# The causal mask of an attention layer cut to its two diagonal squares

## What is computed

```python
def causal_block_attention(q, k, v):
    nb = S_ // Q_BLOCK                       # 256 // 128
    def one_block(args):
        qi, bi = args
        s = jnp.einsum('bqhd,bkhd->bhqk', qi, k).astype(jnp.float32) * scale
        qpos = bi * Q_BLOCK + jnp.arange(Q_BLOCK)
        s = jnp.where(kpos[None, :] <= qpos[:, None], s, -jnp.inf)
        p = jax.nn.softmax(s, axis=-1).astype(v.dtype)
        return jnp.einsum('bhqk,bkhd->bqhd', p, v)
```

## Time and profile before

| | us |
|---|---|
| median of 3 runs | 2367.28 |
| lowest and highest | 2366.36, 2370.49 |
| the profiled execution | 2367.2 |
| its span, first to last instruction | 2365.5 |
| TensorE busy | 2327.2 |
| VectorE busy | 1439.8 |
| ScalarE busy | 1064.5 |

### The profile page before, as it was taken

How to read it: one execution, slowest core, us unless ns; L and a number is a source line. 1 busy time by engine, 2 the same in 40 slices (tenths; PEclk the granted TensorE clock), 3 DMA queues, 4 the chain that set the end, 5 groups by cost and what they waited for, 6 DMA issues and landing times.

```text
span 2365.5 us, 37140 instructions
## 1 busy us (share of the span) xinstructions
PE 2327.2 (98%) x14529; PEld 2024.2 (86%) x14535; DVE 1439.8 (61%) x1559; ACT 1064.5 (45%) x1372; POOL 223.3 (9%) x231
## 2 busy tenths in 40 slices
PE   8999989999999999999999999998999999999999
PEld 7898878888888888888989899887888888888887
DVE  6664567556546556567667767565755555555556
ACT  4455454434434434445544536344443443443442
POOL 0052001001001001000012211110100000000000
PEclk9999999999999999999999999999999999999999
DMA  6664456665665665655533435254666656656654
GB/s 235 195 170 123 148 192 199 200 192 184 196 189 183 198 195 179 199 201 169 171 117 117 145 89 170 85 183 152 196 191 193 189 192 190 191 190 231 187 193 137
DMA packets 236683, 417.25 MB, mean 176 GB/s; under 512 B 23761, under 2 KB 46570, under 8 KB 234986
## 3 DMA queue, kind: packets, MB, share of 16 engines
q1 hardware_dynamic: 235162, 410.73, 55.5%
q10 hardware_dynamic: 1360, 4.19, 0.5%
HBM read 412.77 MB, written 2.10 MB: 175 GB/s over the span
## 4 chain that ended last, share of the span: by engine, by line
PE 90%; DVE 5%; ACT 2%; issue 1%; POOL 1%; DMA 0%; ACTq 0%; POOLq 0%; DVEq 0%
PE quad L642 20%; PE quad L667 13%; PE quad L668 13%; PE quad L669 13%; PE quad L645 10%; PE quad L613 4%; PE quad L615 4%; PE quad L617 4%; DVE wlo L1685 1%; DVE cv L2146 1%; ACT whi L1263 1%; PE quad L1136 1%; PE quad L720 1%; PE quad L810 1%; PE quad L884 1%
## 5 line engine op out<-in xcount | busy, mean ns | idle before, releaser
L1685 DVE TENSOR_TENSOR wlo<-raw,whi 128x1024 fp32r<-128x1024 f32 x760 | 979.2, 1296 | 688.6 <-ACT whi L1263 686.5
L1263 ACT ACTIVATE whi<-raw 128x1024 fp32r<-128x1024 f32 x760 | 800.5, 1058 | 972.9 <-PE quad L669 495.8
L642 PE MATMUL quad<-xs,whi 128*128 128x512 f32 x2048 | 649.3, 397 | 7.1 <-DVE xs L2006 6.2
L667 PE MATMUL quad<-whi,hh 128*128 128x512 f32 x1248 | 488.7, 392 | 1.0 <-POOL hl L2363 1.0
L669 PE MATMUL quad<-whi,hl 128*128 128x512 f32 x1248 | 485.8, 389 | 0.0
L668 PE MATMUL quad<-wlo,hh 128*128 128x512 f32 x1248 | 485.7, 389 | 0.0
L645 PEld LDWEIGHTS quad<-xs,wlo 128*128 128x128 f32 x2048 | 386.8, 189 | 91.4 <-issue 0.3
L645 PE MATMUL quad<-xs,wlo 128*128 128x256 f32 x2048 | 404.0, 279 | 0.6 <-issue 0.6
L642 PEld LDWEIGHTS quad<-xs,whi 128*128 128x128 f32 x2048 | 314.4, 190 | 9.1 <-issue 7.3
L667 PEld LDWEIGHTS quad<-whi,hh 128*128 128x128 f32 x1248 | 234.3, 188 | 49.7 <-POOL hl L2363 1.4
L669 PEld LDWEIGHTS quad<-whi,hl 128*128 128x128 f32 x1248 | 234.3, 188 | 49.3
(11 more groups left out here) (320 smaller groups left out, 2123.5 us busy)
## 6 DMA issues: line engine op xcount, KB each, us to landing
raw<-in_mlp_w SPq DMA_DIRECT2D x512, 512.0 KB
raw<-in_gdn_w_in SPq DMA_DIRECT2D x105, 512.0 KB
raw<-in_w_out SPq DMA_DIRECT2D x64, 512.0 KB
raw<-in_mem_w_kv SPq DMA_DIRECT2D x32, 512.0 KB
raw<-in_mla_w_in SPq DMA_DIRECT2D x25, 512.0 KB
raw<-in_mla_w_ukv SPq DMA_DIRECT2D x24, 256.0 KB
gb<-in_ln_g SPq DMA_DIRECT2D x4, 1024.0 KB, 7.0
gb<-in_ln_b SPq DMA_DIRECT2D x4, 1024.0 KB, 9.1
```

Of the source, the lines that this page charges most:

```text
L642: last = nc.tensor.matmul(both, b.whi[:, slot, k, cols], b.xs[:, :, kt, :], start=start, stop=stop, skip_group_check=True)
L667: nc.tensor.matmul(ps[:, t, 0:n], ah[:, kt, toks], hi[:, k, 0:n], start=start, stop=False)
L1263: nc.scalar.activation(b.whi[:, c % NSPLIT], b.raw[:, slot], ACT.Copy).then_inc(sem.hi_ready, 1)
L1685: nc.vector.tensor_tensor(b.wlo[:, c % NSPLIT], b.raw[:, c % NRAW], b.whi[:, c % NSPLIT].bitcast(F32), ALU.subtract).then_inc(sem.lo_ready, 1)
```

## The change

The mask `causal` shrinks from 128 x 2 x 256 to one square of 128 x 128, the same for both tiles, as each tile's diagonal square is the same. In `scores` the mask is added by two matmuls per head, each over the 128 columns of a tile's diagonal square, the second one between the scores of tile 0 and tile 1. The square of tile 0 by keys 128 to 255 is no longer written. A new function `keys` gives how many keys a tile has, and maximum, exponential and division of tile 0 take 128 instead of 256 columns in causal heads; the maximum becomes one reduction per tile there.

```diff
+def keys(n, t):
+
+    return (t + 1) * P if NM <= n < NM + NH else S
...
-    b.causal, o = at("causal", [P, TT, S], BF16, o)
+    b.causal, o = at("causal", [P, P], BF16, o)
...
-                if causal:
-                    nc.tensor.matmul(ps[:, :], b.identb[:, :], b.causal[:, :, :].rearrange("p t s -> p (t s)"),
-                                     start=True, stop=False, skip_group_check=True)
                 for t in range(TT):
                     toks = slice(t * P, (t + 1) * P)
                     nk = P * (t + 1) if causal else S
+                    if causal:
+                        nc.tensor.matmul(ps[:, t * S + nk - P:t * S + nk], b.identb[:, :], b.causal[:, :], start=t == 0,
+                                         stop=False, skip_group_check=True)
...
                 for t in range(TT):
-                    last = nc.scalar.activation(b.prob[:, n % 2, t, :], turn_ps[n % 2][:, t * S:(t + 1) * S], ACT.Exp,
+                    k = keys(n, t)
+                    last = nc.scalar.activation(b.prob[:, n % 2, t, 0:k], turn_ps[n % 2][:, t * S:t * S + k], ACT.Exp,
...
-                nc.vector.tensor_reduce(b.mx[:, n % 2, :], turn_ps[n % 2][:, :].rearrange("p (t s) -> p t s", t=TT), AX.X,
-                                        ALU.max, negate=True).then_inc(sem.bias_set, 1)
+                if keys(n, 0) == S:
+                    nc.vector.tensor_reduce(b.mx[:, n % 2, :], turn_ps[n % 2][:, :].rearrange("p (t s) -> p t s", t=TT), AX.X,
+                                            ALU.max, negate=True).then_inc(sem.bias_set, 1)
+                    return
+                for t in range(TT):
+                    last = nc.vector.tensor_reduce(b.mx[:, n % 2, t:t + 1], turn_ps[n % 2][:, t * S:t * S + keys(n, t)], AX.X,
+                                                   ALU.max, negate=True)
+                last.then_inc(sem.bias_set, 1)
...
                 for t in range(TT):
-                    last = nc.vector.tensor_scalar(b.prob[:, n % 2, t, :], b.prob[:, n % 2, t, :],
+                    k = keys(n, t)
+                    last = nc.vector.tensor_scalar(b.prob[:, n % 2, t, 0:k], b.prob[:, n % 2, t, 0:k],
                                                    b.rinv[:, n % 2, t:t + 1], None, ALU.mult)
...
-            link(nc.gpsimd.memset(b.causal[:, :, :], 0.0))
+            link(nc.gpsimd.memset(b.causal[:, :], 0.0))
```

More of the change, by code:

```diff
@@ L2351, in _ @@
                     nc.gpsimd.engine_nop().then_inc(sem.const_set, 1)
-            link(nc.gpsimd.memset(b.causal[:, :, :], 0.0))
-            link(nc.gpsimd.affine_select(out=b.causal[:, :, :], in_=b.causal[:, :, :], compare_op=ALU.is_ge, fill=NEG,
-                                         base=0, pattern=[[P, TT], [-1, S]], channel_multiplier=1))
+            link(nc.gpsimd.memset(b.causal[:, :], 0.0))
+            link(nc.gpsimd.affine_select(out=b.causal[:, :], in_=b.causal[:, :], compare_op=ALU.is_ge, fill=NEG,
+                                         base=0, pattern=[[-1, P]], channel_multiplier=1))
             freq = 1.0 / (np.float32(ROPE_THETA) ** (np.arange(0, ROPE, 2, dtype=np.float32) / np.float32(ROPE)))
```

## The result

The changed kernel takes 2372.39 us (median of 22 executions, 2369.60 to 2377.34), the kernel before, timed beside it, 2368.18 (22, 2366.14 to 2370.49). The ratio is 1.0021, 95% interval 1.0014 to 1.0028: slower by 4.2 us (3.3 to 6.6 by the interval), just over the 0.2% that I had called the limit of "no change", and above my range, which ended at 2370.0. Its profiled execution took 2370.82 us, with a span of 2369.1, 3.6 more than before.

What follows compares the result with a forecast made beforehand. TensorE's queue was taken as the bound (busy 98% of the span); masks at -0.06 to +0.06 us and all other parts at nothing summed to 0.0 us, so 2367.2 us, range 2365.0 to 2370.0.

Steps and rivals of the forecast that it cites:

- the limit of "no change": Whole kernel: about 0.2% (4.7 us) is what a measurement can tell from no change; chance of staying within, 0.92.
- The bound of the stage: Twelve causal heads: bound by TensorE's steps, busy 75.34 of 76.00 us, with only a 0.2 us weight-load wait.
- The price of the masks: Causal heads, TensorE: 24 small masks at 0.104 to 0.109 us replace twelve at 0.213; net -0.06 to +0.06 us.
- Rival (a): Causal heads: each small mask costs only its own columns, 0.053 us, giving 2365.9 us; chance 0.25.
- Rival (b): Causal heads: the bf16-to-fp32 weight switch is not hidden, 0.34 us per mask, +5.7 us, giving 2372.9; chance 0.03.
- Maximum, exponential, division: Causal heads, VectorE and ScalarE: changed work lies beside TensorE's path and turns into waiting; counted as no time.
- Rival (d): Freed ScalarE and VectorE time reaches the end after all, at most 5.0 us, giving 2362.2; chance in full 0.01.
- One causal step still 5.24 us long: Expected sign in the changed profile: the distance from one causal head's step to the next stays 5.24 us.
- the 0.1 us of the forecast: Causal-head stage: main forecast of no difference beyond 0.1 us; chance 0.58.
- nothing in the trace depends on an address: Buffers behind `causal` move down 768 bytes a partition; no row prices this, so it was taken as zero.
- The signs of failure: Total off over 3 us with unchanged steps: clock or outside-stage reasoning wrong; step shorter by over 0.1 us: weight-load bound wrong.
- The clock, rival (c): Half-clock stretches after layer norms may shift over other work, -2.1 to +1.3 us each; chance of visible shift 0.11.

Runs made afterwards that it cites:

- vec_only: Changed kernel with TensorE's old 512-column mask and old mask buffer, keeping the new maximum, exponential and division; 2368.57 us, ratio 1.0004 to the kernel before.
- b_pad24: Kernel before with 48 satisfied waits (24 instructions) added ahead of TensorE's first matmul; 2372.30 us, ratio 1.0018.
- a_pad16: Changed kernel with 32 satisfied waits (16 instructions) added ahead of TensorE's first matmul; 2372.13 us, ratio 1.0017 to the kernel before.
- a_pad32: Changed kernel with 64 satisfied waits (32 instructions) added ahead of TensorE's first matmul; 2367.50 us, ratio 0.9995 to the kernel before.

## Why the prediction was wrong

- **The bound of the stage** was right: TensorE at 75.45 of 76 us, no new wait.
- **The price of the masks** was right: 0.11 us each, the scores of a head 0.005 us longer, where I had -0.005 to +0.005. Rival (a), its own columns only, is false where fp32 weights follow, and true where bf16 weights do. Rival (b), a switch that isn't hidden, is false: 0.11 and not 0.34 us. Its total of 2372.9 is near the measured 2372.39 by luck, for a reason that isn't there.
- **Maximum, exponential, division** at nothing was right: `vec_only` 1.0004 [0.9995, 1.0013], and the saved time stands in ScalarE's wait, 2.76 against 2.61 us. Rival (d) is false.
- **"One causal step still 5.24 us long"** was wrong by a little: it became 5.28. The excess is not in the masks but in the 12 matmuls of the output chunk behind them, which take 230 ns from start to start instead of 227. It makes 0.26 us from the first head's mask to the last one's (68.20 against 67.94), more than the 0.1 us of the forecast.
- **The step that failed** is the one that isn't there. I costed each edit in its own stage and at the buffers wrote that "nothing in the trace depends on an address". The address that counts is that of the code. The sum left out that 24 instructions more on TensorE move everything behind them, up to two loops 400 and 1700 us later. In the profiles that costs 0.8 us at the first loop and 2.3 at the second, and `b_pad24`, which has this shift and nothing else of the change, takes 2372.30. In the profile of before this was to be seen: the jump back in the first layer has idle time by "issue", 0.64 us at it and 0.57 us some 19 loads behind it, and the page has the queue that moves instructions. A further rival, code that moves behind the masks, could have been named from them; the records of before would have priced it: the eleven and twelve pairs that the shift takes from behind the jumps last 1.97 and 2.09 us there, so about 2 us at each loop if the fetches come when they came. The runs show 0.8 and 2.3; in the first layer the fetch came 3.1 us behind the one before it, not 4.6.
- **The signs of failure** that I had named did their work: a total off by more than 3 us with steps that keep their length was to mean the clock or "something outside the stage", and it did.
- **The clock, rival (c)**, isn't the cause: in the two profiled executions the half-speed stretches are the same, 6.8 us at each norm, as in the earlier trace rows. But it may enlarge the effect, as the next paragraph says.

What stays open: the profiled stops differ by (1.61 - 0.85) + (2.71 - 0.45) = 3.0 us between the kernels while the medians differ by 4.2; the distances over a stop vary (0.45 and 2.15 us for the same code place), and I have no distribution of them. The mean granted clock, which is on record for each timed execution, points at a part of the rest. The changed kernel's executions at 0.997 (7, the profiled one among them) took 2370.2 us on the mean, those at 0.996 (11) 2373.4, those at 0.994 and 0.995 (4) 2376.5; `b_pad24` has 2369.6 at 0.997 and 2373.3 at 0.996. The kernel before, timed beside `b_pad24`, has 2368.2 at 0.997, 2367.9 at 0.996 and 2369.9 at 0.995. So the place of the code costs less in executions at the highest clock than in the others, as it would if TensorE at times fell to half speed behind a long stop, as in the profile of `a_pad16`. No profile of the changed kernel shows such a fall, so this is not shown. The timed runs of the kernels with stops after few loads spread more (2369.6 to 2377.3) than those of `a_pad32` (2365.1 to 2369.1), which fits, but isn't a proof.

## What to carry to other kernels

Count the instructions that a change adds on an engine whose code is fetched while it runs, and look at every loop's jump back behind it: a change that is neutral where it stands can cost microseconds there, and a gain of that size can be nothing else either. Before you believe a difference of 0.2%, shift the code of the kernel before by as many harmless instructions, or align the loops in both, and compare again. Where the profile says "issue" behind a jump, or names a releaser that had long been done, look at the records of the queue that moves instructions: a stop that each time ends at the same distance behind the end of a fetch points to the code.

## What the runs showed of the hardware

- TensorE's code came in fetches of 16384 bytes, 256 instructions, mostly 0.9 to 1.4 us long beside the weight stream (up to 2.3), 123 in the program. The long stops stood behind the jumps back. There the next fetch began 3.0 to 4.9 us after the one before it (1998.58 and 2001.90 in the changed kernel), and with 2 loads to cover it TensorE was held for 2.7 to 3.0 us, with 8 for 1.6 to 1.9, with 14 for 0.45 to 2.15, with 56 instructions of shift not at all. With the end of a fetched piece inside the head of the loop it was 3.8 us.
- The held load came 1.3 to 1.6 us behind the recorded end of the fetch in each of these stops, and the first load behind a jump 1.7 to 1.9 us behind the end of its fetch. A loop's start at a multiple of 256 instructions took away the stop behind the jump, not the 0.6 to 1.9 us of the jump.
- Behind the stop of 3.8 us the granted clock was 0.50 for 3.4 us; behind those of up to 3.0 us, in the other profiles, it stayed at 1.00.
- The stops came back after the same numbers of loads at a shift of 256 instructions.
- A bf16 matmul of 128 columns took 0.056 us with bf16 weights (the same identity again) loaded behind it and 0.11 us with fp32 weights. This bears on the Trainium skill, page "TensorE: Matmul & The Clock Gate": its section on LDWEIGHTS gives one rule, columns divided by 1.2 GHz (estimate: 107 ns for 128 columns), which the trace agrees with for fp32 weights (loads 0.11 us apart). The bf16 loads are shown 0.10 us long, near the rule too, but two of them stood 0.06 us apart (220.57, 220.63), so that they didn't hold the matmuls to it. Its section on the back-to-back gap gives about 56 ns for an isolated matmul of 128 columns, which fits the bf16 masks, and about 81 ns for a sustained pair of load and matmul, which was not seen for either.
- fp32r matmuls of 512 columns ran at 227 ns from start to start in the output chunks with one or three masks ahead in the head, and at 230 with two or four (the step with three took 5.307 us, where 5.280 + 0.056 = 5.336 would be due at 230). I have no cause for it; masks of odd and even number are all that was varied.
